# Experts' stage: the weight stream issued first on SyncE, eleven small transfers issued by GpSimd

## The reference, cut to what matters

```
def moe(h, w_router, b_router, w1, b1, w2, b2):
    xf = h.reshape(T, D)                                  # T = 256, D = 1024
    logits = xf @ w_router + b_router                     # 32 experts
    top_val, top_idx = lax.top_k(logits, 4)
    gates = softmax(top_val)
    ...                                                   # each expert e gets the tokens that chose it
        u = xb @ w1[e] + b1[e]                            # w1[e]: 1024 x 2048
        glu = minimum(u[:, ::2], 7)
        lin = clip(u[:, 1::2], -7, 7)
        a = glu * sigmoid(1.702 * glu) * (lin + 1)
        return a @ w2[e] + b2[e]                          # w2[e]: 1024 x 1024
    ...                                                   # times its gate, summed over a token's 4 experts
```

## Time and profile before

| | |
|---|---|
| times of three runs | 2033.08, 2039.28, 2041.47 us, median 2039.28 |
| time of the profiled execution | 2032.84 us |
| its span, first to last instruction | 2030.9 us |
| busy share of the span: PE, PEld, DVE, ACT, POOL | 91%, 60%, 37%, 27%, 1% |
| mean granted clock of TensorE | 0.96 of full speed |
| bytes moved | 592.99 MB, 292 GB/s over the span |
| the experts' stage | from about 390 to 1363 us of the span |

### The profile page before, as it was taken

One profiled execution on the slowest core, in us unless ns is written; L12 is line 12 of the kernel. 1 busy time (PEld: TensorE's weight loads), 2 busy tenths in 40 slices (PEclk: granted clock), 3 DMA queues, 4 the chain that ended last, 5 costly groups with the idle time before them and its releaser, 6 DMA issues. The chain is left out here.

```text
span 2030.9 us, 25177 instructions
## 1 busy us (share of the span) xinstructions
PE 1858.0 (91%) x10314; PEld 1212.4 (60%) x10315; DVE 752.9 (37%) x1082; ACT 552.4 (27%) x812; POOL 11.8 (1%) x23
## 2 busy tenths in 40 slices
PE   7999998789999999999999999969889997979998
PEld 6799876633333333333333333328779987868996
DVE  6767643431111111111111111106555555555555
ACT  4444554210000000000000000005544434534442
POOL 0000000000000000000000000000000000000000
PEclk7999998789999999999999999989989998988999
DMA  9877632299999999999999999958335545324552
GB/s 340 310 252 245 232 125 73 98 379 428 431 432 431 431 431 431 432 430 432 430 432 430 432 431 432 431 195 295 125 125 187 187 146 207 123 90 162 183 172 102
DMA packets 152474, 592.99 MB, mean 292 GB/s; under 512 B 7603, under 2 KB 82527, under 8 KB 127824
## 3 DMA queue, kind: packets, MB, share of 16 engines
q1 hardware_dynamic: 150176, 583.90, 72.8%
q0 software_dynamic: 2224, 8.04, 1.1%
HBM read 590.84 MB, written 1.07 MB: 291 GB/s over the span
## 5 line engine op out<-in xcount | busy, mean ns | idle before, releaser
L1419 PE MATMUL psum<-expert_ring,expert_arena 128*64 128x512 f32 x2048 | 454.3, 597 | 21.4 <-DMA expert_ring<-in_w_mlp_dram 21.4
L1419 PEld LDWEIGHTS psum<-expert_ring,expert_arena 128*64 128x64 f32 x2048 | 142.3, 137 | 317.1 <-issue 272.8
L318 DVE TENSOR_TENSOR layer_w_lo<-layer_ring,layer_w_hi 128x1024 fp32r<-128x1024 f32 x190 | 231.4, 1224 | 244.7 <-ACT layer_w_hi L313 244.5
L313 ACT CAST layer_w_hi<-layer_ring 128x1024 fp32r<-128x1024 f32 x190 | 197.8, 1047 | 245.2 <-PE psum L363 127.3
L1435 PE MATMUL psum<-expert_ring,expert_arena 128*64 128x512 f32 x1024 | 234.7, 602 | 29.5 <-DMA expert_ring<-in_w_mlp_dram 29.5
L361 PE MATMUL psum<-layer_x_hi,layer_w_hi 128*128 128x256 f32 x864 | 249.0, 288 | 11.1 <-DVE layer_w_lo L318 8.1
L362 PE MATMUL psum<-layer_x_lo,layer_w_hi 128*128 128x256 f32 x864 | 247.8, 287 | 0.0
L363 PE MATMUL psum<-layer_x_hi,layer_w_lo 128*128 128x256 f32 x864 | 247.7, 287 | 0.0
L1308 DVE TENSOR_SCALAR expert_arena<-psum 128x512 f32<-128x512 f32 x32 | 22.1, 692 | 557.0 <-PE psum L1419 557.0
L361 PEld LDWEIGHTS psum<-layer_x_hi,layer_w_hi 128*128 128x128 f32 x864 | 169.4, 196 | 13.7 <-issue 9.8
L1435 PEld LDWEIGHTS psum<-expert_ring,expert_arena 128*64 128x64 f32 x1024 | 68.6, 137 | 176.2 <-issue 117.9
(11 more groups left out here) (274 smaller groups left out, 1987.8 us busy)
## 6 DMA issues: line engine op xcount, KB each, us to landing
expert_ring<-in_w_mlp_dram SPq DMA_DIRECT2D x192, 2048.0 KB, 23.4
layer_ring<-in_w_ffn_in_dram SPq DMA_DIRECT2D x44, 1024.0 KB, 5.0
mixer_ring<-in_w_in_dram SPq DMA_DIRECT2D x38, 1024.0 KB, 5.8
mixer_ring<-in_w_ada_dram SPq DMA_DIRECT2D x24, 1024.0 KB, 5.7
layer_ring<-in_w_ffn_out_dram SPq DMA_DIRECT2D x20, 1024.0 KB, 4.9
layer_ring<-in_b_w_in_dram SPq DMA_DIRECT2D x10, 1024.0 KB, 7.4
layer_ring<-in_w_mix_out_dram SPq DMA_DIRECT2D x8, 1024.0 KB, 4.9
layer_ring<-in_a_w_in_dram SPq DMA_DIRECT2D x7, 1024.0 KB, 8.3
```

Source lines behind the costliest of these rows:

```text
L313: self.nc.scalar.copy(hi, raw).then_inc(self.hi_ready, 1)
L318: self.nc.vector.tensor_tensor(lo, raw, hi.bitcast(FP32), ALU.subtract).then_inc(self.lo_ready, 1)
L1419: last = nc.tensor.matmul(U[CAP * h:CAP * h + CAP, N * n:N * n + N], xg[:, k, j, :], ring[:, at:at + N], start=False, stop=k == KC - 1)
```

## The change

The eleven small transfers leave SP's list, so that its first instruction in the block is the first 2 MiB weight transfer. GpSimd gets a list of its own, which issues them in a new order (`wr`, `br`, then the table, then the biases) and waits for all of them at its end. Their semaphores and those who wait on them stay the same.

```
-            sp.dma_start(M["later"][:, :], A["table_later"]).then_inc(row_here, 16)
-            sp.dma_start(wr, A["w_router"][0].rearrange("(k p) e -> p k e", p=P)).then_inc(row_here, 16)
-            sp.dma_start(br.unsqueeze(1), A["b_router"][0:1, :].partition_broadcast(P)).then_inc(row_here, 16)
-            for h in range(2):
-                for part in range(2):
-                    r = CAP * h + E * part
-                    sp.dma_start(bias_raw[r:r + E, 0:D], A["b_mlp1"][0, :, D * h:D * h + D]).then_inc(bias_here, 16)
-                    sp.dma_start(bias_raw[r:r + E, D:D + N], A["b_mlp2"][0, :, N * h:N * h + N]).then_inc(bias_here, 16)
...
             one_round(0)
             further_rounds(sp, one_round)
+
+        @block.gpsimd
+        def _(pool):
+            pool.dma_start(wr, A["w_router"][0].rearrange("(k p) e -> p k e", p=P)).then_inc(row_here, 16)
+            pool.dma_start(br.unsqueeze(1), A["b_router"][0:1, :].partition_broadcast(P)).then_inc(row_here, 16)
+            pool.dma_start(M["later"][:, :], A["table_later"]).then_inc(row_here, 16)
+            for h in range(2):
+                for part in range(2):
+                    r = CAP * h + E * part
+                    pool.dma_start(bias_raw[r:r + E, 0:D], A["b_mlp1"][0, :, D * h:D * h + D]).then_inc(bias_here, 16)
+                    pool.dma_start(bias_raw[r:r + E, D:D + N], A["b_mlp2"][0, :, N * h:N * h + N]).then_inc(bias_here, 16)
+            pool.wait_ge(row_here, 48)
+            pool.wait_ge(bias_here, 16 * 8)
```

## The result

| | before | after |
|---|---|---|
| median of six runs | 2033.6 us (2029.6 to 2041.5) | 2046.6 us (2043.1 to 2052.6) |
| ratio, 95% interval | | 1.0064 [1.0049, 1.0079] |
| span of the profiled execution | 2030.9 us | 2041.3 us |
| experts' stage, its first issue to the next stage's | 973.0 us | 983.3 us |

The change makes the kernel slower by 13 us (10 to 16). One of the nine executions of a later kernel (reorder) fell in a slower state at 2129 us, and its ratio leaves it out. The mixer's length varies from one execution to the next (the experts' stage begins at 387.4 to 393.1 us in the traces of this case, the mixer being the same in all), so from here on times in the stage are counted from its first issue, written +10.8: 390.60 us in the trace of before, 387.44 after.

A forecast was written before the change was run, and what follows sets the result against it. The experts' weight stream at 431 GB/s bounds the kernel, from the refill that the router's chain sets. No gain plus a +4 us delay: 2032.84 + 4 = 2036.8, on the median's scale 2039.3 + 4 = 2043 us; range 2035 to 2055.

The forecast's parts named there:

- What bounds the stage: Experts' stage: its end moves with the refill issue at 429.27 us, set by the router's chain, not the first weights.
- The gain: none: First weight issue 5.2 us earlier is worth nothing; ring full at about 425 only lengthens the idle time before the refill.
- Issue on POOL: POOL's issues: about 0.9 us for wr, 0.55 for each of ten others, all issued by 397.0; they cost nothing.
- A turn is a weight packet; POOL's queue joins rows: DMA engines: each small packet's turn costs 0.61 us; POOL joins rows up to at least 4 KB, wr being 2 packets.
- turns of whole transfers: Rival, DMA queues: a newcomer waits out the 2 MiB transfer in work, 4.9 us each time; +11.5, 2051 us; chance 0.10.
- The sum of row_here: Router's rows: 390.6 + 5.4 + 10 x 0.61 + 1.8 = 403.9 us, delaying TensorE 0 to 4.3 us, 2.5 by the middle.
- 5.4: POOL's first transfer: us from issue to landing under a running stream, taken as the start and holding the first packet's turn.
- The sum of the biases: Bias_here 9.1 to 14.0 us after row_here, 413.0 to 417.9; past 413.3 it delays DVE's subtraction, 0 to 4.6 us.
- The forecast of +4, at most +6: Everything from the gather on: the later of the rows' and biases' delays counts, +4 us, bounds 0 and about +6.
- The hole near the second expert: DMA engines from 451 to 453 us, 0.59 busy: can gain or lose a microsecond or two with TensorE's clock.

The follow-up runs named there:

- reorder: Against the kernel before: the biases on POOL's queue, rows first on SP, banks cleared early, expert 0's tokens chosen before DVE's subtraction; ratio 0.9973.
- wait_all: The changed kernel, with SP waiting until all eleven small transfers have landed before its first weight transfer; ratio 0.9998 against the kernel before.
- rows_sp: The changed kernel with the three row transfers back on SP ahead of the weights, biases still on POOL; ratio 1.0000 against the kernel before.
- reorder_before: The kernel before with banks cleared early and tokens chosen before the subtraction, all eleven small transfers ahead of the weights on SP; ratio 0.9971.
- wr_act: The changed kernel with the router's weights issued from ACT's queue, on their own semaphore; one run, stage 1003.7 us.
- short_packets_2: The changed kernel with expert 0's weights in 8 KB rows and TensorE waiting for each ring slot by itself; one run, stage 976.6 us.
- br_sp: The changed kernel with the router's broadcast bias alone back on SP ahead of the weights, with its own semaphore; one run, stage 982.4 us.
- rows_pool: The changed kernel with the eight biases back on SP ahead of the weights, the three row transfers still on POOL; one run, stage 972.9 us.

## Why the prediction was right in sign and range, and wrong in size

- *What bounds the stage.* Right. The refill's first issue moved by 10.9 us and the stage's end by 10.3. wait_all starts the stream 5.4 us later than before and loses nothing, rows_sp 3.7 us earlier and gains nothing.
- *The gain: none.* Right: rows_sp, and as far as it goes reorder against reorder_before. The ring was not full at about 425 as I wrote (+34.4) but at +41: the stream is slowed by what flows beside it (373 GB/s from 397 to 427 us, where before it had 418).
- *Issue on POOL.* Right: 0.90 us for wr, 5.9 us for all eleven.
- *A turn is a weight packet; POOL's queue joins rows.* Right, by the 544 packets, by wr_act (627 against 627) and by short_packets_2. The rival "turns of whole transfers" falls with the table: 8 packets and a semaphore write in the 6.6 us after br's landing (399.2 to 405.8), 0.73 us a turn, not 4.9. The rule of the Trainium skill weighed there (DMA: Bandwidth & Descriptors, "Queues, rings and completion order": typically 9 to 17 descriptors to a packet) doesn't hold for the weights' queue; each of its 16 KB rows was a turn by itself.
- *The sum of row_here, mis-sized.* I put it at 13.3 us after the stage's start, at most 15.1; it was 18.4. Of the 5.1 us, 2.3 are wr's: it landed at +8.7, 0.45 + 8.2, where 5.4, a turn and its bytes make 6.3. Another 2.5 are br's: 3.1 us behind wr where a turn of 0.6 was allowed, since I put br's own time at nothing. The table took 6.6 us, forecast 6.3.
- *The sum of the biases, mis-sized.* I took 9.1 to 14.0 us after row_here; it was 16.4. The semaphore writes do count as turns, and a turn is 0.79 us of weight packet and not 0.61 while 32 neighbouring partitions are written (20 of these are 15.8 us, which with 1.8 us of bytes is 1.2 too much; 12 of them are 5.1 too few). That slowing was in the trace of before: from 391 to 397 us the same biases went at 229 GB/s, and I read it as a gap that the weights could fill.
- *Together.* The forecast of +4, at most +6 by its own bounds, was +10.9. The joints were all later than forecast: in before's times the product at 409.0 (forecast 403 to 406), the cast at 425.4 (413 to 418), the refill at 440.2 (432 to 436). The step that failed is the sum behind "I take +4 us": its ceiling lacked br's own time and the slower turns beside 32-partition writes, and wr came later than its 5.4 us. That 2043 us stood close to the measured 2046.6 is luck: the median of before, from which it was counted, was 2039.3 after three runs and 2033.6 after six.
- *The hole and the clock.* The hole near the second expert stayed. TensorE stood idle for 7.44 us before the product, at a mean granted clock of 0.57 from 397 to 427 us (0.63 before), mostly the lower level, 1.2 GHz; its bank clearing (5.46 us) and gather took about as long as before. The clock did cost something in br_sp, reorder and reorder_before, where the gather ran near the lower level.

## What to carry to other kernels

A small transfer that someone waits for belongs ahead of a bulk stream in the same queue, or gets a head start: beside the stream, every packet of it waits for a bulk packet, so its price goes by its count of packets (semaphore writes too) times the length of the bulk packets, more than by its bytes. That priced the table and the biases well; the first packet waited some 3 us more, and the broadcast had a time of its own. Before starting a stream earlier, look whether its end or its first refill is what anyone waits for: here the buffer was full in time either way. Eight transfers of 32 neighbouring partitions are a bad shape for this; spread over all partitions, or with shorter packets in the bulk stream while they flow, they cost less. And when work leaves the path of TensorE, look at the granted clock behind it: here the bank clearing kept it up for the gather.

## What the runs showed that I had not expected

- Writes to 32 neighbouring partitions slow not only themselves but the traffic beside them: a 16 KB packet took 0.79 us beside them and 0.61 beside the same bytes spread over all partitions.
- Moving the first weight issue by 3.6 us made the rows' delay vanish, from 7.6 us to none (rows_pool; counted from POOL's first issue).
- The broadcast of 128 bytes to 128 partitions cost 3.1 us of the product's start beside the stream, and landed 1.9 us after wr without one; ahead of the weights on SP's queue it landed in 3.5.
- A shortened chain lost 3.3 us of its gain because the gather, no longer right behind the bank clearing, ran at the lower clock (7.5 us of matmuls instead of 4.2).
- GpSimd's subtraction stopped DVE: 4.03 us instead of 0.92 for four operations that touch 32 elements of each partition.
